# Further rows as plain-type products in four column tiles, their gate/up product between the high and the low down products, and weight loads that wait for a product

## The chip, the cores and the metric

The kernel runs on one core of one Trainium2 chip. The metric is the time of one execution on the device, in microseconds, as the median of several runs. The engines are TensorE (PE; its weight loads are shown as PEld), VectorE (DVE), ScalarE (ACT), GpSimd (POOL) and SyncE (SP), which here only issues transfers.

## The reference

One decoder layer on 1024 tokens of width 1024: forgetting attention with 16 heads, a residual with LayerNorm, and a mixture of 64 routed experts and one shared one, cut here to what the change touches:

```python
# router: sigmoid scores, 4 of 8 groups, 8 of 64 experts a token, weights scaled by 2.5
# expert e, on the tokens routed to it:
h = silu(x @ w_gate[e]) * (x @ w_up[e])      # 1024 -> 256
y = (h @ w_down[e]) * weight                 # 256 -> 1024
# shared expert: the same with ws_gate, ws_up, ws_down, on all tokens
x = layer_norm(alpha * x + shared + sum_of_routed, g, b)
```

All inputs, outputs and weights are float32.

## The kernel before, in words

**The stages.** Attention, output projection with LayerNorm and router, then the shared expert in eight blocks of 128 tokens, then the 64 routed experts in order, then the last placing of rows and the second LayerNorm. Each routed expert takes one block of 128 token rows; tokens beyond that come in *further* blocks of XR = 32 rows. With this data 31 of the 64 experts have one further block and 33 have none (`nx` is 1 or 0). The code for more than one is there and is skipped.

**The products.** The first 128 rows are computed in a split form: weights and rows are each a high and a low part of type fp32r, and a product is three matmuls, high·high, low·high, high·low. `gate_up` has 24 matmuls of 512 columns (L1032, L1035, L1038), `down` has 12 (`down_hi` L1059, L1060, then `down_lo` L1067). ScalarE makes the high parts of the weights (L1404), VectorE the low parts (L1926). Before the change the further rows use the same split weights: `xo` (and `ho`) hold the high part of the rows in columns 0 to 31, the low part in 32 to 63 and zeros behind, so one matmul gives both; `gate_up_further` has 16 matmuls (L1091, L1092), `down_further` 8 (L1109, L1110). Halves are then added by ScalarE and VectorE (`further_half` L1499, `further_sum`, `further_y_half`, `further_y`).

**The order of one expert e on TensorE.** With a further block in expert e-1: turn_h (L1046, transposes of the hidden rows of the block before), gate_up, turn_h_further (L1100), the transposes of the next rows (L1022), down_further. Then, with a further block in e: turn_further (L1081), down_hi and down_lo of the block before, gate_up_further. Without it: down_hi and down_lo only. ScalarE, in its own order: L1499 for the further block before, ht_hi (L1440), silu of the further rows (L1503), four casts of the gate/up weights of set e+2 (L1404), ho (L1507), silu (L1436), the next rows (L1432), the copy of the further result, xo (L1494), two casts of down weights, and `scale_rows` (L1452), which scales the block's result out of `k_ps`. At every even expert ScalarE, VectorE and TensorE load block counts from memory into registers (`load_counts`, L1522 on ScalarE).

**The loads.** Weights of set s (0 the shared expert, s = e+1 for expert e) are loaded in six pieces of 512 KB by SyncE: four of gate/up (L500) and two of down (L505), into two buffers each. A piece is issued when VectorE is done with the piece in the same buffer:

```python
load_gate_up(par, *(... w_gate, w_up), lambda k: sp.wait_ge(S["g_lo_ok"], G_PIECES * (s - 2) + k + 1))
load_down(par, ..., lambda k: sp.wait_ge(S["d_lo_ok"], D_PIECES * (s - 2) + k + 1))
```

GpSimd gathers the 128 (and 32) token rows of an expert by index (L664, L677) and adds the results back into memory (L689, L699). Each engine runs its experts in a loop of two experts a turn, apart from the first and last ones on some engines.

`gate_sums` (L812), which the rows below show, is an older part of the kernel: 20 plain float32 matmuls of 256 or 128 columns and 16 output rows, in four column tiles of TensorE, which hold two, four, six and eight of them (384, 896, 1408 and 1920 columns).

Of the kernel before, what the change touches and what calls it, by code (L numbers as in the profile page):

```python
# [84 lines left out]
I32 = mybir.dt.int32  # L85
U32 = mybir.dt.uint32
# [9 lines left out]
def build(nc, x, w_in, b_f, w_out, ln1_g, ln1_b, router, router_bias, w_gate, w_up, w_down, ws_gate, ws_up,  # L96
          ws_down, ln2_g, ln2_b, out):
    with ExitStack() as ctx:
# [135 lines left out]
        with ExitStack() as m:  # L234

            raw_gu = [sb(f"raw_gu{i}", [P, 2, DC, FF], c=m) for i in range(2)]
# [4 lines left out]
            xo = sb("xo", [P, DC, P], F32R, c=m)  # L241
            ho = sb("ho", [P, FC, P], F32R, c=m)
            gu_x = sb("gu_x", [XR, 2 * FF], c=m)
            ys = [sb(f"ys{i}", [P, D], c=m) for i in range(3)]
            sg = sb("sg", [P, FF], c=m)
            hh = sb("hh", [P, FF], c=m)
            ht_hi = sb("ht_hi", [P, FC, P], F32R, c=m)
            ht_lo = sb("ht_lo", [P, FC, P], F32R, c=m)
            w_x = sb("w_x", [XR, 1], c=m)
            wcol = sb("wcol", [P, E], c=m)  # L250
            gidx = [sb(f"gidx{i}", [P, 1], I32, c=m) for i in range(3)]
            sidx = [sb(f"sidx{i}", [P, 1], I32, c=m) for i in range(3)]
            sb("to_64_bytes", [P, 8], c=m)
            split = []
# [3 lines left out]
            tab = sb("tab", [P, TAB], I32, c=m)  # L258
            tok_f = sb("tok_f", [P, 1], c=m)
            tok_x = sb("tok_x", [2 * XR, 1], c=m)  # L260
        with ExitStack() as f:

            fin0 = sb("fin0", [P, TT, D], c=f)
            y_hi = sb("y_hi", [P, D], F32R, c=f)
            y_lo = sb("y_lo", [P, D], F32R, c=f)
            tokens = sb("tokens", [P, T], c=f)
            x_place = sb("x_place", [2 * XR, T], F32R, c=f)
# [12 lines left out]
            sb("up_to_the_other_set", [P, 19240], c=f)  # L280
            fin1 = sb("fin1", [P, TT, D], c=f)

# [3 lines left out]
        for n in ("masks xt_ps xt_hi_ok xt_lo_ok wf_in wf_ok gate_ps g1_in gate_step zexp_ok"  # L286
# [7 lines left out]
                  " ht_lo_ok downed scaled w_ok x_in x_turned x_rows_hi_ok x_rows_lo_ok x_w_ok x_gated x_half x_sum x_silu_ok x_h_ok x_ht_ps x_ht_hi_ok x_ht_lo_ok"  # L294
                  " x_downed x_y_half x_scaled ax_ok ax_stored summed"
                  " stands std_ok var_ok place_step y_hi_ok f_placed f_pair f_mean f_var f_std f_scaled f_step f_xg f_out").split():
# [52 lines left out]
        def g_piece(w, k):  # L349

            return tuple(a[:, k // 2, (k % 2) * 4:(k % 2) * 4 + 4, :] for a in (raw_gu[w], split[w][0], split[w][1]))

        def d_piece(w, k):
            return tuple(a[:, k, :] for a in (raw_dn[w], split[w][2], split[w][3]))

# [31 lines left out]
        def _(sp):  # L387
# [106 lines left out]
            def load_gate_up(par, gate, up, left):  # L494

                for k in range(G_PIECES):
                    left(k)
                    chunks = slice(k % 2 * (DC // 2), (k % 2 + 1) * (DC // 2))
                    w = (gate, up)[k // 2].rearrange("(p c) n -> p c n", c=DC)[:, chunks]
                    sp.dma_start(raw_gu[par][:, k // 2, chunks], w).then_inc(g_raw[par][k // 2], 16)  # L500
# [6 lines left out]
            def next_gate_up(s, par):  # L507

                load_gate_up(par, *(w[ds(s - 1, 1)].rearrange("o k n -> (o k) n") for w in (w_gate, w_up)),
                             lambda k: sp.wait_ge(S["g_lo_ok"], G_PIECES * (s - 2) + k + 1))  # L510

            def next_down(s, par):
                load_down(par, w_down[ds(s - 1, 1)].rearrange("o k n -> (o k) n"),
# [28 lines left out]
            for b in range(2, SH):  # L542
# [5 lines left out]
                elif b == 5:  # L548
                    next_gate_up(2, 0)
                elif b == 6:  # L550
                    next_down(2, 0)
# [3 lines left out]
            sp.dma_start(tab[:], tab_dram.rearrange("(p n) o -> p (n o)", p=P)).then_inc(S["c_loads"], 16)  # L555


            next_gate_up(3, 1)
# [4 lines left out]
            next_gate_up(E, 0)  # L563
            next_down(E - 1, 1)
            next_down(E, 0)

# [11 lines left out]
            for t in range(2):  # L578
                load_sums(0, t)
# [1582 lines left out]
```

## Time and profile before

| | |
|---|---|
| median of 3 runs | 1641.52 us (1641.01 to 1644.18) |
| the profiled execution | 1632.95 us, span 1631.3 us, mean clock of TensorE 0.979 |
| TensorE busy | 1574.2 us, 97% of the span |
| VectorE, ScalarE, GpSimd busy | 1183.2, 1033.3, 505.7 us |
| expert stage | from about 744 to 1568 us, then some 63 us |
| moved by the DMA queues | 368.63 MB |

An engine that waits in order for semaphores is shown idle, and the one that released it is named. TensorE's matmuls are pipelined: the starts of two neighbours are 0.227 us apart in a 512-column product, while each is shown as 0.39 us long; so starts are what to read. Times in the rows are microseconds from the start of the span, unless marked ns.

### The profile page before, as it was taken

What the parts mean: (1) busy time and instruction counts of PE and PEld (TensorE: products, weight loads), DVE (VectorE), ACT (ScalarE), POOL (GpSimd) and SP (SyncE); (2) the same over time, 40 slices, a digit from 0 to 9 for tenths busy, and PEclk for the clock granted to TensorE, in tenths of its full rate; (3) what the DMA queues carried; (4) which work ended last, traced back from release to release, by engine and by line L of the source; (5) the groups of instructions that cost most, each with busy time, mean ns of one, the idle gap of its engine ahead of it and who ended that gap; (6) DMA issues with size and microseconds to landing.
All of it is one profiled execution on the core that took longest, in us unless ns stands there. A gap on an engine that the chain in (4) does not pass through costs nothing.

```text
span 1631.3 us, 32225 instructions
## 1 busy us (share of the span) xinstructions
PE 1574.2 (97%) x8262; PEld 1310.3 (80%) x8263; DVE 1183.2 (73%) x2038; ACT 1033.3 (63%) x1709; POOL 505.7 (31%) x495
## 2 busy tenths in 40 slices
PE   6999999999999999899999999999999999999987
PEld 6997888888887788788888888788888888888864
DVE  4215777777777788838777888767876787888856
ACT  3215666666666645427667877766776777877855
POOL 0000000000000135532544454543554455454426
PEclk9999999999999999899999999999999999999995
DMA  7223222212223524568999999999998999999987
GB/s 247 91 82 96 67 59 65 71 45 71 58 65 111 185 108 170 196 218 315 318 303 309 304 363 360 329 289 263 331 322 276 286 356 326 348 365 370 366 252 283
DMA packets 161319, 368.63 MB, mean 226 GB/s; under 512 B 53008, under 2 KB 73488, under 8 KB 161264
## 3 DMA queue, kind: packets, MB, share of 16 engines
q1 hardware_dynamic: 136272, 284.21, 49.9%
q0 software_dynamic: 24992, 83.73, 19.8%
q8 instruction: 28, 0.46, 0.1%
q14 instruction: 27, 0.22, 0.0%
HBM read 294.39 MB, written 65.11 MB: 220 GB/s over the span
## 4 chain that ended last, share of the span: by engine, by line
PE 78%; DVE 7%; issue 4%; ACT 3%; DMA 3%; ACTq 2%; POOL 1%; SPq 0%; DVEq 0%; POOLq 0%
PE bank_pair L1032 6%; PE bank_pair L1035 6%; PE bank_pair L1038 6%; PE q_ps L91 4%; PE out_ps L923 4%; PE q_ps L93 4%; PE q_ps L92 4%; PE k_ps L901 4%; PE out_ps L1091 4%; PE out_ps L1092 3%; PE q_ps L1022 3%; PE k_ps L1059 3%; PE k_ps L1060 2%; PE k_ps L1067 2%; DVE gu_lo L1926 2%
## 5 line engine op out<-in xcount | busy, mean ns | idle before, releaser
L1926 DVE TENSOR_TENSOR gu_lo<-raw_gu,gu_hi 128x1024 fp32r<-128x1024 f32 x260 | 306.4, 1219 | 28.7 <-ACT gu_hi L1404 28.7
L1404 ACT CAST gu_hi<-raw_gu 128x1024 fp32r<-128x1024 f32 x260 | 253.3, 1050 | 6.0 <-DMA raw_gu<-in_moe_w_up_dram 6.0
L1032 PE MATMUL bank_pair<-gu_hi,xb_hi 128*128 128x512 f32 x576 | 235.5, 409 | 5.4 <-DVE gu_lo L1926 4.2
L1035 PE MATMUL bank_pair<-gu_lo,xb_hi 128*128 128x512 f32 x576 | 229.1, 398 | 0.0
L689 POOL DMA_INDIRECT sums_scratch<-ys,sidx x63 | 119.8, 1902 | 151.7 <-DMA sums_scratch<-ys,sidx 110.6
L1926 DVE TENSOR_TENSOR dn_lo<-raw_dn,dn_hi 128x1024 fp32r<-128x1024 f32 x130 | 152.6, 1213 | 2.2 <-ACT dn_hi L1404 1.7
L1038 PE MATMUL bank_pair<-gu_hi,xb_lo 128*128 128x512 f32 x576 | 142.7, 390 | 0.0
L1032 PEld LDWEIGHTS bank_pair<-gu_hi,xb_hi 128*128 128x128 f32 x576 | 111.5, 194 | 29.5 <-issue 6.5
L1309 ACT CAST pt_hi<-k_ps 128x512 fp32r<-128x512 f32 (+1 forms) x192 | 85.9, 482 | 74.2 <-PE k_ps L901 73.4
L620 POOL IOTA e<- 128x64 f32 x1 | 0.2, 185 | 426.6 <-DVE xs L1722 426.6
L1404 ACT CAST dn_hi<-raw_dn 128x1024 fp32r<-128x1024 f32 x130 | 130.0, 1051 | 3.2 <-DMA raw_dn<-in_moe_w_down_dram 3.2
L1035 PEld LDWEIGHTS bank_pair<-gu_lo,xb_hi 128*128 128x128 f32 x576 | 111.0, 193 | 21.6
L1038 PEld LDWEIGHTS bank_pair<-gu_hi,xb_lo 128*128 128x128 f32 x576 | 108.0, 188 | 22.9 <-DVE xb_lo L1930 0.5
L664 POOL DMA_INDIRECT x_rows<-rows_scratch,gidx x64 | 74.7, 1167 | 148.2 <-DVE wcol L1942 117.5
L1700 DVE TENSOR_TENSOR pt_lo<-k_ps,pt_hi 128x512 fp32r<-128x512 f32 (+1 forms) x192 | 100.3, 550 | 27.5 <-ACT pt_hi L1309 26.6
L1059 PE MATMUL k_ps<-dn_hi,ht_hi 128*128 128x512 f32 x288 | 118.4, 411 | 0.0
L1060 PE MATMUL k_ps<-dn_lo,ht_hi 128*128 128x512 f32 x288 | 112.5, 391 | 0.0
L91 PE MATMUL q_ps<-xt_hi,wqk_hi 128*128 128x512 f32 x256 | 108.8, 425 | 0.0
L1298 ACT ACTIVATE probs<-bank_pair,nm 128x512 f32<-128x512 f32 (+3 forms) x128 | 74.9, 587 | 42.4 <-DVE nm L1693 29.0
L1091 PE MATMUL out_ps<-gu_hi,xo 128*128 128x512 f32 x248 | 97.2, 392 | 4.5 <-DVE xo L1946 4.5
L93 PE MATMUL q_ps<-xt_hi,wqk_lo 128*128 128x512 f32 x256 | 100.2, 391 | 0.0
L92 PE MATMUL q_ps<-xt_lo,wqk_hi 128*128 128x512 f32 x256 | 100.0, 391 | 0.0
(306 smaller groups left out, 3971.5 us busy)
## 6 DMA issues: line engine op xcount, KB each, us to landing
raw_gu<-in_moe_w_gate_dram SPq DMA_DIRECT2D x128, 512.0 KB, 6.6
raw_gu<-in_moe_w_up_dram SPq DMA_DIRECT2D x128, 512.0 KB, 9.1
raw_dn<-in_moe_w_down_dram SPq DMA_DIRECT2D x128, 512.0 KB, 8.9
wqk<-in_fox_w_in_dram SPq DMA_DIRECT2D x66, 128.0 KB, 2.4
v_scratch<-v_out SPq DMA_DIRECT2D x32, 256.0 KB, 2.8
va<-v_scratch SPq DMA_DIRECT2D x16, 512.0 KB, 4.7
fin<-sums_scratch SPq DMA_DIRECT2D x16, 512.0 KB, 9.0
xs<-in_x_dram SPq DMA_DIRECT2D x8, 512.0 KB, 7.8
```

Of the source, the lines that this page charges most:

```text
L91: pe.matmul(out, w_hi, m_hi, start=start, stop=False, skip_group_check=True)
L92: pe.matmul(out, w_hi, m_lo, start=False, stop=False, skip_group_check=True)
L93: return pe.matmul(out, w_lo, m_hi, start=False, stop=stop, skip_group_check=True)
L689: g.indirect_dma_start(out=sums[0], out_offset=bass.IndirectOffsetOnAxis(ap=sidx[par][:, 0:1], axis=0), in_=ys[par][:], in_offset=None, co ...
L1032: i = pe.matmul(o3, xb_hi[s][:, c], g_hi[:, :, c], start=c == 0, stop=False, skip_group_check=True)
L1035: pe.matmul(o3, xb_hi[s][:, c], g_lo[:, :, c], start=False, stop=False, skip_group_check=True)
L1038: i = pe.matmul(o3, xb_lo[s][:, c], g_hi[:, :, c], start=False, stop=c == DC - 1, skip_group_check=True)
L1059: pe.matmul(k_ps[:, r], ht_hi[:, c], d_hi[:, c, r], start=c == 0, stop=False, skip_group_check=True)
L1060: pe.matmul(k_ps[:, r], ht_hi[:, c], d_lo[:, c, r], start=False, stop=False, skip_group_check=True)
L1091: pe.matmul(o3, xo[:, c], g_hi[:, :, c], start=c == 0, stop=False, skip_group_check=True)
L1404: a.copy(hi, raw).then_inc(S[done], 1)
L1926: dve.tensor_tensor(lo, raw, hi, ALU.subtract).then_inc(S[lo_ok], 1)
```

## The change

The further rows are no longer split. `xo` and `ho` are float32 with 32 columns, the weights are read unsplit from the load buffers, and each product is cut over four column tiles of 32 output rows: gate and up, each in even and odd chunks of the inner dimension; for down two chunks by two halves of the columns. `gate_up_further` stands between `down_hi` and `down_lo`. VectorE's low parts of the further rows are gone; the adds of halves are two of half the width. Since unsplit weights are now read late, gate/up load buffers are three, and two waits are added on SyncE, `gu_spent` (counted by TensorE in its first low down product of an expert with a further block, in its first high one without) and `downed`. The memory for the third buffer comes from tiles that are shared: hh becomes sg, the third `ys` lies in `x_rows2`, and the index table is int16, copied by GpSimd from the third up buffer. The loops of TensorE, ScalarE, VectorE and SyncE have six experts a turn, ten turns, with the first two and last two experts outside.

```diff
-            raw_gu = [sb(f"raw_gu{i}", [P, 2, DC, FF], c=m) for i in range(2)]
+            raw_gu = [[sb(f"raw_{n}{i}", [P, DC, FF], c=m) for n in ("gate", "up")] for i in range(2)]
...
-            xo = sb("xo", [P, DC, P], F32R, c=m)
-            ho = sb("ho", [P, FC, P], F32R, c=m)
+            xo = sb("xo", [P, DC, XR], c=m)
+            ho = sb("ho", [P, FC, XR], c=m)
...
+        def raw_place(s):
+
+            return s if s < 2 else (0, 2, 1)[(s - 2) % 3]
...
+        ROUND = 6
+        ROUNDS = (E - 4) // ROUND
...
+            def next_gate_up(s, place):
+
+                if place > 3:
+                    sp.wait_ge(S["gu_spent"], s - 3)
+                    stand(sp)
...
+            def next_down(s, place):
+                if place > 2:
+                    sp.wait_ge(S["downed"], SH + s - 2)
+                    stand(sp)
...
-            with sp.Fori(0, E // 2 - 2) as i:
-                for par in range(2):
-                    next_gate_up(2 * i + (par + 4), par)
-                    next_down(2 * i + (par + 3), 1 - par)
...
+            with sp.Fori(0, ROUNDS) as i:
+                for u in range(ROUND):
+                    next_gate_up(ROUND * i + (u + 4), u + 4)
+                    next_down(ROUND * i + (u + 3), u + 3)
...
-                for c in range(DC):
-                    pe.matmul(o3, xo[:, c], g_hi[:, :, c], start=c == 0, stop=False, skip_group_check=True)
-                    i = pe.matmul(o3, xo[:, c], g_lo[:, :, c], start=False, stop=c == DC - 1, skip_group_check=True)
+                for c in range(0, DC, 2):
+                    for j in range(4):
+                        i = pe.matmul(out_ps[x_tile(j), BANK:BANK + FF], xo[:, c + j // 2], raw[j % 2][:, c + j // 2], start=c == 0,
+                                      stop=c == DC - 2, skip_group_check=True)
...
+            def down_further(e, s, x, by_rows=True):
+
+                raw = raw_dn[s % 2]
+                pe.wait_ge(S["x_ht_ok"], x + 1)
+                pe.wait_ge(d_raw[s % 2], 8 * D_PIECES * (e + 1 - s % 2) + 16 * D_PIECES)
+                stand(pe)
+                for j in range(4):
+                    c, half = (j // 2, j % 2) if by_rows else (j % 2, j // 2)
+                    i = pe.matmul(out_ps[x_tile(j), BANK:T], ho[:, c], raw[:, c, HALVES[half]], start=True, stop=True, skip_group_check=True)
...
-                    down(m - 1, par, e + 1)
+                    down_hi(m - 1, par, e + 1)
+                    if not last:
+                        gate_up_further(u + 1, xi + nx - 1)
+                    down_lo(m - 1, par, spent=not last)
...
-                a.copy(gu_x[:], out_ps[XR:2 * XR, BANK:T]).then_inc(S["x_half"], 1)
+                a.copy(gu_x[:, 0:FF], out_ps[x_tile(2), BANK:BANK + FF]).then_inc(S["x_half"], 1)
+                a.copy(gu_x[:, FF:2 * FF], out_ps[x_tile(3), BANK:BANK + FF]).then_inc(S["x_up_half"], 1)
```

**On TensorE**, in the code of an expert with a further block, after its transposes (k_ps takes the down product of the block before, out_ps the further rows). Before:

```order
L1081 MATMUL bank_pair<-ident,x_rows 128x32 x8
L1054 REGISTER_ALU
L1056 REGISTER_ALU
L1059 MATMUL k_ps<-dn_hi,ht_hi 128x512
L1060 MATMUL k_ps<-dn_lo,ht_hi 128x512
...
L1067 MATMUL k_ps<-dn_hi,ht_lo 128x512 x4
L1091 MATMUL out_ps<-gu_hi,xo 128x512
L1092 MATMUL out_ps<-gu_lo,xo 128x512
```

and now:

```order
L1120 MATMUL bank_pair<-ident,x_rows 128x32 x8
L1094 MATMUL k_ps<-dn_hi,ht_hi 128x512
L1097 MATMUL k_ps<-dn_lo,ht_hi 128x512
...
L1130 MATMUL out_ps<-raw_gate,xo 32x256
L1130 MATMUL out_ps<-raw_up,xo 32x256
L1104 MATMUL k_ps<-dn_hi,ht_lo 128x512 x4
L1239 UNCONDITIONAL_BRANCH
```

The pairs at the "..." repeat, four of the down product in both, and eight of L1130, which stood as eight pairs L1091, L1092 behind L1067 before. L1067 (now L1104) ends the part.

**On SyncE**, in the loop over the experts' loads, between gate/up of one set and down of the set before. Before:

```order
L500 DMA raw_gu<-in_moe_w_up_dram 128x1024 [waits g_lo_ok]
L514 ISA
L505 ISA [waits d_lo_ok]
L505 DMA raw_dn<-in_moe_w_down_dram 128x1024
L514 REGISTER_ALU
L505 ISA [waits d_lo_ok]
L505 DMA raw_dn<-in_moe_w_down_dram 128x1024
L510 ISA
L500 ISA [waits g_lo_ok]
L500 DMA raw_gu<-in_moe_w_gate_dram 128x1024
```

and now:

```order
L523 DMA raw_up<-in_moe_w_up_dram 128x1024 [waits g_lo_ok]
L540 REGISTER_ALU
L543 ISA [waits downed]
L528 ISA [waits d_lo_ok]
L528 DMA raw_dn<-in_moe_w_down_dram 128x1024
L543 REGISTER_ALU
L528 ISA [waits d_lo_ok]
L528 DMA raw_dn<-in_moe_w_down_dram 128x1024
L536 ISA [waits gu_spent]
L523 ISA [waits g_lo_ok]
L523 DMA raw_gate<-in_moe_w_gate_dram 128x1024
```

The order of the loads is the same; a wait for `downed` now stands ahead of the down pieces and one for `gu_spent` ahead of the gate/up pieces. They are issued in the order down of set s, then gate/up of set s+2, both after the end of expert s-2.

## Rows read from the trace of the kernel before

**Rows 1.** The page, part 1: busy us (share of the span) xinstructions.
```profile
PE 1574.2 (97%) x8262; PEld 1310.3 (80%) x8263; DVE 1183.2 (73%) x2038; ACT 1033.3 (63%) x1709; POOL 505.7 (31%) x495
```

**Rows 2.** Windows: stretch, us, busy of five engines, PEclk, DMA share, GB/s.
```profile
764.00:1567.00 803.00, 790.90 (x3826) 652.14 (x3826) 630.84 (x786) 587.23 (x757) 382.45 (x363) 1.00 1.00 327
1484.80:1542.40 57.60, 56.57 (x278) 47.50 (x277) 50.71 (x58) 48.59 (x59) 25.20 (x23) 1.00 1.04 367
1590.00:1620.00 30.00, 28.57 (x64) 16.47 (x63) 21.25 (x38) 18.00 (x27) 25.96 (x12) 0.58 0.71 280
```

**Rows 3.** Timeline of PE: start us, us, operation, count [idle before].
```profile
1032.92 0.39 PE L1046 MATMUL bank_pair<-ident,hh 128*128 128x128 f32 x2
...
1206.32 0.39 PE L1091 MATMUL out_ps<-gu_hi,xo 128*128 128x512 f32 x1
...
1209.95 0.39 PE L1046 MATMUL bank_pair<-ident,hh 128*128 128x128 f32 x2
...
1217.01 0.48 PE L1109 MATMUL out_ps<-dn_hi,ho 128*128 128x512 f32 x1
...
1219.04 1.06 PE L1081 MATMUL bank_pair<-ident,x_rows 32*128 32x32 f32 x8
...
1226.52 0.39 PE L1046 MATMUL bank_pair<-ident,hh 128*128 128x128 f32 x2
```

**Rows 4.** Groups of 764:1567: shapes xcount, busy us, mean ns, idle before.
```profile
L1091 PE MATMUL out_ps<-gu_hi,xo 128*128 128x512 f32 x240 | 94.0, 392 | 4.5 <-DVE xo L1946 4.5
```

**Rows 5.** Waits of 764:1567: us in total, times, longest us.
```profile
ACT gu_x L1499 <- PE out_ps L1092: 73.0, 30, 3.3
...
ACT ht_hi L1440 <- issue: 27.5, 13, 2.3
...
PEld out_ps L1091 <- DVE xo L1946: 6.6, 5, 1.5
```

**Rows 6.** Timeline of PE around gate_sums.
```profile
71.27 0.28 PE L93 MATMUL bank_pair<-wv_hi,xt_lo 128*128 128x256 f32 x1
71.48 3.44 PE L812 MATMUL q_ps<-upto,gate 128*16 128x256 f32 x40
74.84 0.39 PE L91 MATMUL bank_pair<-wv_hi,xt_hi 128*128 128x256 f32 x1
75.07 0.28 PE L92 MATMUL bank_pair<-wv_lo,xt_hi 128*128 128x256 f32 x1
```

**Rows 7.** Timeline of ACT in three experts.
```profile
1033.40 1.12 ACT L1452 ACTIVATE ys<-k_ps,wcol 128x1024 f32<-128x1024 f32 x1
1036.58 0.37 ACT L1440 CAST ht_hi<-bank_pair 128x256 fp32r<-128x256 f32 x1 [2.06 <-issue]
...
1206.77 1.12 ACT L1452 ACTIVATE ys<-k_ps,wcol 128x1024 f32<-128x1024 f32 x1 [0.94 <-PE k_ps L1067]
1210.15 0.58 ACT L1499 COPY gu_x<-out_ps 32x512 f32<-32x512 f32 x1 [2.26 <-PE out_ps L1092]
...
1211.80 3.89 ACT L1404 CAST gu_hi<-raw_gu 128x1024 fp32r<-128x1024 f32 x4
1216.20 0.21 ACT L1507 CAST ho<-out_ps 128x64 fp32r<-128x64 f32 x1 [0.51 <-PE out_ps L1100]
```

**Rows 8.** Timeline of SP's queue: start us, us of issuing.
```profile
1206.69 1.47 SPq L505 DMA_DIRECT2D raw_dn<-in_moe_w_down_dram  x2
1214.29 1.43 SPq L500 DMA_DIRECT2D raw_gu<-in_moe_w_gate_dram  x2
```

**Rows 9.** Instruction queues (page, part 3), and one wait of 690:800.
```profile
q8 instruction: 28, 0.46, 0.1%
q14 instruction: 27, 0.22, 0.0%
...
PEld bank_pair L1046 <- issue: 1.0, 1, 1.0
```

**Rows 10.** Waits of 1567:1632.
```profile
POOL fin L783 <- DMA fin<-sums_scratch: 9.0, 3, 8.2
```

More of the change, by code:

```diff
@@ L85 @@
 I32 = mybir.dt.int32
+I16 = mybir.dt.int16
 U32 = mybir.dt.uint32
@@ L492, in _, with load_gate_up @@
                 weights_out(t - 1)
[L494 removed]
+            def load_gate_up(place, gate, up, left):
                 for k in range(G_PIECES):
@@ L1170, in _, with expert @@
                     logits(TT - 1)
-            def expert(e, par, last=False):
+            def expert(e, u, last=False):
+                par = u % 2
                 w = 1 - par
@@ L1215, in expert @@
                         turn_h_further(xi + nx - 1)
-                        down_further(w, e + 2, xi + nx - 1)
+                        down_further(e, u + 1, xi + nx - 1, by_rows=False)
                         put_in_place(True)
                 with pe.If(nx < 1):
-                    down(m - 1, par, e + 1)
+                    down_hi(m - 1, par, e + 1, spent=not last)
+                    down_lo(m - 1, par)
                     if last:
@@ L1224, in expert @@
                 return xi, nx
-            with pe.Fori(0, E // 2 - 1) as i:
-                for par in range(2):
-                    expert(2 * i + par, par)
-            expert(E - 2, 0)
-            expert(E - 1, 1, last=True)
+            for e in range(2):
+                expert(e, e)
+            with pe.Fori(0, ROUNDS) as i:
+                for u in range(2, ROUND + 2):
+                    expert(ROUND * i + u, u)
+            expert(E - 2, E - 2)
+            expert(E - 1, E - 1, last=True)
         @block.scalar
@@ L1597, in _ @@
             expert(1, 1, "", counts)
-            with act.Fori(1, E // 2 - 1) as i:
-                counts = load_counts(2 * i)
-                for par in range(2):
-                    expert(2 * i + par, par, "", counts)
+            with act.Fori(0, ROUNDS) as i:
+                for u in range(2, ROUND + 2):
+                    if u % 2 == 0:
+                        counts = load_counts(ROUND * i + u)
+                    expert(ROUND * i + u, u, "", counts)
             counts = load_counts(E - 2)
-            expert(E - 2, 0, "", counts)
-            expert(E - 1, 1, "last", counts)
+            expert(E - 2, E - 2, "", counts)
+            expert(E - 1, E - 1, "last", counts)
             for t in range(TT):
@@ L2014, in load_counts, with expert @@
                 return [dve.value_load(earlier[0:1, ds(e + k, 1)], min_val=0, max_val=E * TAB_BLOCKS) for k in range(4)]
-            def expert(e, par, counts, last=False):
+            def expert(e, u, counts, last=False):
+                par = u % 2
                 m = SH + e
```

225 lines of the change are left out of this document (119 added, 106 removed).

## The prediction

> **What bounds the kernel now.** I read first the busy shares on the page, then the windows of the expert stage, then the waits there, and last single timelines. TensorE is busy 97% of the span [rows 1]. In 764 to 1567 us, 61 experts, it is busy 790.9 of 803.0 us at clock 1.00, so what it issues is what the stage costs; the DMA engines read 1.00 there too, at 327 GB/s [rows 2]. An expert starts with the transposes of its hidden rows (L1046). With a further block before it and in it, one lasts from 1209.95 to 1226.52, 16.57 us [rows 3]. Six without a further block take 57.6 us [rows 2], 9.6 each. Thirty-one of the 64 experts have one further block of 32 rows; 30 fall in this window, as the counts of L1091 (240 = 30 x 8) show [rows 4].
>
> The waits are to be read with that: the long ones belong to engines with time to spare. ScalarE waits 73.0 us in 30 times for L1092, then VectorE for ScalarE. TensorE waits for almost nothing: 6.6 us of weight loads for VectorE's low parts of the further rows [rows 5]. So shorter TensorE work pays only until the spare time of ScalarE and of the DMA queues is used up, and that is where I look.
>
> **What is taken from TensorE.** gate_up_further was 16 matmuls of 512 columns: it starts at 1206.32 and the next expert's work at 1209.95, 3.63 us. down_further is 8 at the same pace: from 1217.01, 8 x 0.227 = 1.8 us, and with the slow first ones 2.03 by the start of the next transposes, 1219.04 [rows 3]. Now they are plain-type matmuls, 16 of 256 columns and 4 of 512, in four column tiles of 32 rows. The trace has one place with that shape: gate_sums (L812), where 20 plain matmuls stand in four column tiles, the longest tile holding seven of 256 columns and one of 128, 1920 columns. It takes 3.44 us from 71.48, and the next product begins at 74.84 [rows 6]. All four tiles hold 384 + 896 + 1408 + 1920 = 4608 columns; one after the other at the longest tile's pace that would be about 8 us, so the tiles run side by side, and a column costs 3.36 / 1920 = 1.75 ns in its tile. The gate/up block has 4 x 256 columns a tile: 1.79 us. The down block has 512: 0.90. To each I add about 0.25 us for changing over: before L812 a gap of 0.09 more than the pace, after it a first product of 0.39 against 0.28 us. So 2.03 for 3.63 and 1.15 for 2.03: 2.48 us for each of 30, **-74.4 us**. VectorE's low parts of xo go as well, and the five waits for them: **-4.5** by TensorE's idle time [rows 4].
>
> The Trainium skill, "TensorEngine Tiling (Array Packing)", section on performance, speaks against taking the ideal: changing tile modes drains the array, and quoted speed-ups stay under the number of tiles. This trace agrees in kind (the slow first product of rows 6). Its page "TensorE: Matmul & The Clock Gate" gives 2.38 for three column tiles; were four tiles to give about 3 of 4, an estimate from that page, the two blocks would cost 2.4 and 1.2 us with the changeover counted in, and 12 us of the gain would go.
>
> **What ScalarE gets in return.** Before, the last low down products come ahead of gate/up of the further rows, so the scaling of the result rows (L1452, 1.12 us) runs at 1206.77, 3.2 us before the expert ends, under the further products; then ScalarE waits 2.26 us for them [rows 7]. Now down_lo stands last, and L1452 can start only some 0.45 us into the next expert, as it does already where no further block is: 1033.40, with that expert's start at 1032.92 [rows 3, 7]. Behind it stand, in ScalarE's order: the loads of four block counts into registers in every even expert (from the end of L1452 to L1440 2.06 us at 1036.58, in all 27.5 us in 13 times [rows 5, 7]); the half copies of gate/up; the high part of the hidden rows; silu; four casts of gate/up weights, 3.89 us; and only then ho, the turned further hidden rows, for which down_further waits. Ho starts at 1216.20, 6.25 us into the expert, and TensorE wants it at 1217.01, 7.06 us in [rows 3, 7]. After: L1452 ends at 0.45 + 1.12 = 1.57; register loads to 3.65; from the half copy to the first cast is 1.65 us (1210.15 to 1211.80) and the second half copy adds 0.1; the casts end at 5.4 + 3.89 = 9.3; ho at 9.5 (its wait for TensorE's transposes is gone by then). That is 2.3 us late, less what the register loads overlap with: I take 1.9. Of the 30 experts with a block before them 17 are even; in the other 13 ho comes at 7.45, 0.4 late. 17 x 1.9 + 13 x 0.4 = **+38**. Bounds: nothing where TensorE is late for another reason (0), and 17 x 2.4 + 13 x 0.6 = 49.
>
> **What the loads get.** Before, SyncE issued gate/up loads piece by piece as the splits finished, from 1214.29, 4.3 us into an expert, and down loads one expert earlier than they are wanted (1206.69) [rows 8]. Now gate/up for set s waits for gu_spent (the first low down product, the end of expert s-4; a third buffer makes up for it), and down for set s waits for the end of expert s-2, and its cast comes in expert s-1. Behind these waits in SyncE's queue stand only the next loads. Six 512 KB loads are issued in one burst, and down has one expert, less its last 4 us, to land. The bytes: 803 us x 327 GB/s = 263 MB in 61 experts, 4.3 MB each; in 1484.80 to 1542.40 the queues moved 367 GB/s [rows 2]. At that pace 4.3 MB need 11.7 us. On the whole 263 MB fit in 716 us, well under what I forecast; only runs of experts without further blocks, 17 experts in all, ask for more than the queues give, and live on loads issued early. With less issued early, up to 17 x (11.7 - 9.6) = 36 us could come back. The lower bound is 0, since ScalarE's delays lengthen the neighbours; I take a quarter: **+9**.
>
> **The longer loops.** From two experts a turn to six, ten turns. The kernel before fetched 28 + 27 instruction packets in its whole run, and one wait, 1.0 us with no other cause, stands at the start of its loop, L1046 [rows 9]. If a turn has one such stall, it is 10 x 1.0 = **+10**; the bounds are 0 and the rival below.
>
> The rest I cost at nothing: int16 copy of the table on GpSimd, under shared-expert blocks in which its gathers are early; one DVE operation fewer, one more, both under TensorE's 97%. At the end nothing is gained from the last block: the final loads and GpSimd's wait of 9.0 us for them [rows 10] set that part, with the clock at 0.58 [rows 2].
>
> Sum: -74.4 - 4.5 + 38 + 9 + 10 = -22. The profiled execution took 1632.95 us (span 1631.3), the median is 1641.52, 8.6 above; I take the difference off the median: **1619.5 us**.
>
> **Rivals.** (a) The full gain: the queue and ScalarE waits vanish in one another, the loops stay resident: -79, 1563 us. For it: the DMA average leaves room, and TensorE, when it waits for ho, still has eight transposes to do. Against it: ScalarE's order is fixed, and its chain above has no slack. 0.10. (b) The loads bound it: +36 in place of +9, and ho at its upper 49: -79 + 36 + 49 + 10 = +16 as a sum of both uppers, but they overlap in time, so nearer -5 to +5, 1637 to 1646. For it: DMA share 1.00. 0.12. (c) The other side: the loop body of six experts no longer stays in TensorE's instruction store, and each turn fetches it anew. Place: TensorE between two turns and at each jump over a skipped block. Price: 1.0 us for each stall [rows 9]; with eight a turn +80 for +10, so +48, 1690 us. It decides from 32 us of stalls, 3.2 us a turn. For it: three times the instructions a turn. Against: in straight code before 744 us only one such wait is seen. 0.15. The Trainium skill, "Runtime: NRT & Kernel Launch", section on instruction fetch mechanics, says TensorE holds 128 KiB of instructions and that a jump outside what is held stalls; by it six experts would be near or above the limit, two were not. No run here shows the limit. (d) The column tiles don't run side by side: 16 x 0.45 and 4 x 0.9 us in place of 2.03 and 1.15, +7.6 us for each of 30, about +230 against the forecast, near 1850 us. Against it stands all of rows 6. 0.03.
>
> **The numbers.** The forecast has 0.60, with 1600 to 1636 of its own. A change under 0.2% (3.3 us) can't be told from none here. Faster: forecast 0.60, (a) 0.10, half of (b) 0.06. Same: 0.04 of (b). Slower: (c), (d) and the rest of (b). The range from 1583 to 1652 leaves out (a)'s far end, (d), and most of (c).
>
> **What the profile after would show.** The L1130 group: about 1.8 us a block from its start, then k_ps products at once; L1150 about 0.9. L1452 right after an expert's start everywhere. TensorE waiting for ho before L1150, near 2 us in even experts. ScalarE's wait for the further products of 73.0 us gone. DMA above 335 GB/s in the stage. Instruction packets: if many more than 55, (c). I am wrong if ho is hidden, or if waits for raw_dn show in ScalarE by tens of us.

## The result, and the profile after

The change made the kernel slower: 1791.13 us (1785.8 to 1799.69) against 1641.76 us beside it, a ratio of 1.091 [1.086, 1.096]. The prediction was 1619.5 us, faster.

The page of the changed kernel: its span, the busy time, the granted clock by slices, and the two instruction queues.

```profile
span 1785.6 us, 33142 instructions
...
PE 1572.1 (88%) x8758; PEld 1242.8 (70%) x8759; DVE 1182.0 (66%) x2036; ACT 1031.0 (58%) x1741; POOL 431.1 (24%) x496
...
PEclk9999999999999988998998999998899989888996
...
q8 instruction: 147, 2.41, 0.5%
q14 instruction: 123, 1.01, 0.2%
```

Four things are to be seen beside [rows 1, 9]. TensorE is busy about as long as before (1572.1 against 1574.2 us) although it was given some 75 us less to do. Its idle time went from 57 to 214 us. The clock row has many eights where it had nines; its mean is 0.934 against 0.979. And the two instruction queues moved 147 and 123 packets where they had moved 28 and 27. The window of the expert stage says the same beside [rows 2]: the DMA queues move 278 GB/s, not 327, so they are not what holds it.

```profile
764.00:1700.00 936.00, 778.68 (x4250) 577.50 (x4248) 620.72 (x777) 575.23 (x776) 300.55 (x359) 0.91 0.88 278
```

The waits of that stretch (who waited, for whom, us in total, times, the longest) beside [rows 5]:

```profile
ACT ys L1499 <- PE k_ps L1104: 156.4, 43, 8.4
...
PEld bank_pair L1081 <- issue: 92.5, 51, 7.3
...
PE bank_pair L1081 <- issue: 72.4, 42, 6.9
...
PEld k_ps L1094 <- issue: 59.5, 17, 6.7
ACT x_rows L1547 <- issue: 45.9, 17, 7.3
...
PEld bank_pair L1120 <- issue: 27.4, 15, 6.3
```

TensorE's weight loads waited 92.5, 59.5 and 27.4 us for "issue": for nothing that the profile knows, no product, cast or transfer. Its products stood idle for 72.4 us of the first of these (the PE line), and for 24.1 and 14.2 us of the other two. ScalarE's 45.9 us at L1547 are such waits too, together with its register loads. Single waits are long, up to 7.3 us. One on the timeline of the weight loads, with the idle time ahead of it in the last bracket:

```profile
1213.08 0.29 PEld L1094 LDWEIGHTS k_ps<-dn_hi,ht_hi 128*128 128x128 f32 x1 [6.72 <-issue]
```

L1094 is the first product of down_hi, behind the branches round a further block that this expert does not have. The profile names nothing that it still needed. That the instruction itself was missing is the reading that the experiments test.

### The profile page after: what moved, and what is told of

It reads as the page before. It is cut to its first block, busy times and chain, and to the rows that moved or that the text cites. A ratio compares the mean times of both kernels' runs of the same rounds, so it can differ in the third digit from the quotient of the medians.

```text
span 1785.6 us, 33142 instructions
## 1 busy us (share of the span) xinstructions
PE 1572.1 (88%) x8758; PEld 1242.8 (70%) x8759; DVE 1182.0 (66%) x2036; ACT 1031.0 (58%) x1741; POOL 431.1 (24%) x496
## 4 chain that ended last, share of the span: by engine, by line
PE 69%; issue 11%; DVE 8%; DMA 5%; ACT 4%; ACTq 1%; SPq 1%; another core or an unknown queue 1%; DVEq 0%; POOL 0%; POOLq 0%
PE bank_pair L1067 6%; PE bank_pair L1070 6%; PE bank_pair L1073 5%; PE out_ps L958 4%; PE k_ps L1094 4%; PE q_ps L92 4%; PE k_ps L1104 4%; PE q_ps L94 4%; PE q_ps L93 4%; PE k_ps L936 4%; PE k_ps L1097 3%; PE out_ps L1130 3%; DMA raw_up<-in_moe_w_up_dram 3%; PE q_ps L1057 3%; ACT gu_hi L1451 2%
## 5 line engine op out<-in xcount | busy, mean ns | idle before, releaser
L1067 PE MATMUL bank_pair<-gu_hi,xb_hi 128*128 128x512 f32 x576 | 254.5, 442 | 2.8 <-DVE gu_lo L1978 1.5
L1070 PE MATMUL bank_pair<-gu_lo,xb_hi 128*128 128x512 f32 x576 | 245.4, 426 | 8.2 <-issue 8.2
L1978 DVE TENSOR_TENSOR gu_lo<-raw_gate,gu_hi 128x1024 fp32r<-128x1024 f32 x130 | 153.6, 1223 | 34.9 <-ACT gu_hi L1451 32.4
L1094 PE MATMUL k_ps<-dn_hi,ht_hi 128*128 128x512 f32 x288 | 129.3, 449 | 45.7 <-issue 24.1
L1499 ACT ACTIVATE ys<-k_ps,wcol 128x1024 f32<-128x1024 f32 x63 | 70.3, 1116 | 161.1 <-PE k_ps L1104 157.2
L1978 DVE TENSOR_TENSOR gu_lo<-raw_up,gu_hi 128x1024 fp32r<-128x1024 f32 x130 | 158.3, 1219 | 7.5 <-ACT gu_hi L1451 7.4
L1067 PEld LDWEIGHTS bank_pair<-gu_hi,xb_hi 128*128 128x128 f32 x576 | 123.0, 214 | 29.7 <-issue 3.3
L720 POOL DMA_INDIRECT sums_scratch<-ys,sidx x63 | 107.1, 1700 | 150.0 <-ACT ys L1499 76.5
L1451 ACT CAST dn_hi<-raw_dn 128x1024 fp32r<-128x1024 f32 x130 | 129.8, 1049 | 11.5 <-DMA raw_dn<-in_moe_w_down_dram 6.4
L1451 ACT CAST gu_hi<-raw_up 128x1024 fp32r<-128x1024 f32 x130 | 129.6, 1046 | 11.1 <-DMA raw_up<-in_moe_w_up_dram 11.0
L1451 ACT CAST gu_hi<-raw_gate 128x1024 fp32r<-128x1024 f32 x130 | 130.0, 1050 | 7.0 <-DMA raw_gate<-in_moe_w_gate_dram 5.5
L1094 PEld LDWEIGHTS k_ps<-dn_hi,ht_hi 128*128 128x128 f32 x288 | 59.0, 205 | 72.0 <-issue 59.9
L1081 PE MATMUL bank_pair<-ident,sg 128*128 128x128 f32 x144 | 36.9, 343 | 79.6 <-issue 73.6
```

The source lines that it names most:

```text
L720: g.indirect_dma_start(out=sums[0], out_offset=bass.IndirectOffsetOnAxis(ap=sidx[par][:, 0:1], axis=0), in_=ys[par][:], in_offset=None, co ...
L1067: i = pe.matmul(o3, xb_hi[s][:, c], g_hi[:, :, c], start=c == 0, stop=False, skip_group_check=True)
L1070: pe.matmul(o3, xb_hi[s][:, c], g_lo[:, :, c], start=False, stop=False, skip_group_check=True)
L1094: i = pe.matmul(k_ps[:, r], ht_hi[:, c], d_hi[:, c, r], start=c == 0, stop=False, skip_group_check=True)
L1451: a.copy(hi, raw).then_inc(S[done], 1)
L1978: dve.tensor_tensor(lo, raw, hi, ALU.subtract).then_inc(S[lo_ok], 1)
```

## The experiments

The instruction counts below are counted in the built programs, a split-type product or transpose as two instructions (its weight load and its product) and a plain-type product as four, as the trace shows it. The "store theory" of the expectations is rival (c) of the prediction: an engine keeps its recent instructions in a store, and a loop body that is too large for it is fetched again in every turn. For the loop bodies over the experts:

| kernel | TensorE | ScalarE | VectorE |
|---|---|---|---|
| before | 745 | 145 | 165 |
| changed | 2625 | 435 | 493 |

The packets of the first instruction queue (q8) can be set against the size of TensorE's whole program: 28 packets for 7312 instructions before, 34 for 8772 with four experts a turn (experiment 3), 32 for 8319 in the small kernel (experiment 5). That is some 260 instructions a packet, and in these three kernels all code came once.

**1. TensorE without the code of a second further block.** Code that never runs with this data is taken out of the changed kernel:

```diff
-                    with pe.If(nx > 1):
-                        with pe.Fori(0, nx - 1) as k:
...
```

> The changed kernel without TensorE's code for a second or later further block of one expert (no expert of this data has one, so no executed product is left out; the other engines keep theirs). Instructions in TensorE's six-expert loop body, by my count of the built programs: 2625 in the changed kernel, 1941 here, 745 in the kernel before. Store theory (TensorE's loop body no longer stays resident and is fetched anew every turn): if the size that stays resident lies above 1941, instruction packets fall from 270 to near 60-70, TensorE's waits with no cause (92.5 + 59.5 + 27.4 us of weight loads) fall below 20 us, the clock returns to about 0.98, and the time is 1600 to 1640. Load theory (the late weight loads delay the splits and these delay TensorE): nothing changes, 1780 to 1800. Tile theory (plain-type column tiles cost more than I took): nothing changes either.

Measured: 1732.84 us, ratio to before 1.055 [1.053, 1.056]. That is 60 us less than the changed kernel relative to before. Of what is executed only one branch an expert with a further block is gone (31 instructions in all), no product and no load, so neither the load theory nor the tile theory allows it. That branch jumped over the code taken out; this experiment alone does not tell the size of the body from the jump, the next two do. The waits for an instruction at L1094 fell from 59.5 to 20.4 us and at L1120 from 27.4 to 12.9, where the skipped code had stood; those at L1081 rose, from 92.5 to 106.9. The instruction queues are hardly emptier, where I had expected 60 to 70 packets in all:

```profile
q8 instruction: 125, 2.05, 0.5%
q14 instruction: 123, 1.01, 0.2%
```

So the case of a limit above 1941 instructions fell, and with it the 1600 to 1640 us that I had expected; the theory needed a body small enough.

**2 and 3. The kernel before, TensorE's loop at six and at four experts a turn.** Nothing else differs, no product, load or order:

```diff
-            with pe.Fori(0, E // 2 - 1) as i:
-                for par in range(2):
-                    expert(2 * i + par, par)
+            for par in range(2):
+                expert(par, par)
+            with pe.Fori(0, 10) as i:
+                for u in range(2, 8):
+                    expert(6 * i + u, u % 2)
```

> The kernel before, with TensorE's expert loop alone cut into six experts a turn, ten turns, the first two experts outside; all else as before. Its loop body has 2229 instructions by my count. Store theory: slower than before, with long waits of TensorE that have no cause and over 150 instruction packets, by 60 to 150 us, if the limit lies between 1941 and 2229. Load theory and tile theory: the same time as before within 0.5%, since neither loads nor products differ.

> The kernel before, with TensorE's expert loop cut into four experts a turn, fifteen turns: 1487 instructions by my count. Store theory: within 0.3% of before, 55 to 65 instruction packets. A rival within it (the number of experts a turn or the longer straight code costs in itself, by each jump): slower, about two thirds of what six a turn cost.

Six a turn (2229 instructions): 1712.49 us, ratio 1.043 [1.040, 1.046]. Four a turn (1487): 1645.55 us, ratio 1.003 [1.001, 1.005]. Both are as the store theory had them. The pages of six and of four:

```profile
span 1711.0 us, 32148 instructions
...
q8 instruction: 127, 2.08, 0.5%
q14 instruction: 27, 0.22, 0.0%
```

```profile
q8 instruction: 34, 0.56, 0.1%
q14 instruction: 27, 0.22, 0.0%
```

Six a turn moved 99 packets more than before, all on one queue, which is thus TensorE's. The program itself is longer by 2202 instructions, some nine packets; the other 90 are ten for each of the nine times that the loop returns to its start. Four a turn moved 34, no more than its code once. The long waits (3.8 to 6.9 us) stand where the loop turns, shorter ones at later transposes that begin an expert:

```profile
PEld bank_pair L1046 <- issue: 66.3, 21, 6.9
```

This shows the mechanism alone: +69 us from the size of a loop body. The jumps round skipped code are the same in all three kernels, and cost nothing that shows while the body is small. For TensorE the limit lies between 1490 (experiment 5) and 1941 instructions.

**4. The kernel before with gate_up_further between down_hi and down_lo,** in the split form:

```diff
-                    down(m - 1, par, e + 1)
+                    down_hi(m - 1, par, e + 1)
+                    if not last:
+                        gate_up_further(w, xi + nx - 1)
+                    down_lo(m - 1, par)
...
-                    gate_up_further(w, xi + nx - 1)
+                        gate_up_further(w, xi + nx - 1)
```

> The kernel before with gate_up_further of the split form moved between down_hi and down_lo, nothing else. By my prediction's term for ScalarE: the scaling of the result rows (L1452) and the register loads behind it come after the start of the next expert, ho comes 1.9 us late in 17 even experts and 0.4 in 13 odd ones, so 38 us slower, with TensorE waiting for ho before L1109. If that term is wrong: within 0.3% of before.

Measured: 1746.46 us, ratio 1.062 [1.060, 1.065], +103 us where I expected 38. TensorE's waits for ho are there, 30 of them, and each is 1.8 us on the average:

```profile
PE out_ps L1109 <- DVE ho L1964: 54.9, 30, 2.6
```

That is 54.9 us of the 103. Most of the rest can be seen on TensorE's timeline around one of them, and in the windows of the same stretch (PEclk is the third value from the end):

```profile
1206.63 0.79 PE L1109 MATMUL out_ps<-dn_hi,ho 128*128 128x512 f32 x1 [2.61 <-DVE ho L1964]
...
1207.64 0.63 PE L1109 MATMUL out_ps<-dn_hi,ho 128*128 128x512 f32 x1
1208.07 0.63 PE L1110 MATMUL out_ps<-dn_lo,ho 128*128 128x512 f32 x1
...
1212.75 0.39 PE L1059 MATMUL k_ps<-dn_hi,ht_hi 128*128 128x512 f32 x1
1212.98 0.40 PE L1060 MATMUL k_ps<-dn_lo,ht_hi 128*128 128x512 f32 x1
```

```profile
1200.00:1204.00 4.00, 4.00 (x22) 3.08 (x20) 2.62 (x4) 3.47 (x6) 0.87 (x2) 1.00 0.77 125
1204.00:1207.60 3.60, 0.99 (x3) 0.83 (x3) 3.60 (x6) 2.94 (x5) 0.00 (x0) 0.76 0.62 170
1207.60:1212.50 4.90, 4.90 (x13) 3.79 (x12) 2.49 (x4) 1.97 (x3) 1.19 (x2) 0.50 0.88 289
1212.50:1223.00 10.50, 10.50 (x52) 8.79 (x51) 8.98 (x10) 8.53 (x11) 6.57 (x6) 0.99 0.83 253
```

After 3.6 us in which TensorE did little, the clock is 0.50 (1.2 GHz) for 4.9 us: products follow each other at 0.43 us and not 0.23, and then it is whole again. Over the run, the mean clock is 0.953 against 0.979. The clock is granted at 1.2 or 2.4 GHz, so time at half clock is twice the missing share, 2 x 0.047 x 1745.7 = 164 us against 2 x 0.021 x 1631.3 = 69; half of the 95 us more is lost, 48 us. The two profiled executions are 114.4 us apart, since that of before was one of the shorter ones: TensorE's idle time grew by 67.9 us, of which the waits for ho are 54.9, and its busy time by 46.5, near the 48. The remaining 13 us of idle time were not followed up.

**5. The changed kernel made small.** The code of a second further block is out on three engines, and TensorE has one copy of an expert's first half in place of two:

```diff
+                turn_h(m - 1)
+                pe.wait_ge(S["g_lo_ok"], G_PIECES * (e + 2))
+                gate_up(par, w, "rows_", m + 1)
                 with pe.If(before_it > 0):
-                    turn_h(m - 1)
-                    pe.wait_ge(S["g_lo_ok"], G_PIECES * (e + 2))
-                    gate_up(par, w, "rows_", m + 1)
                     pe.wait_ge(S["ht_lo_ok"], m)
                     turn_h_further(xi - 1)
-                    turn_next()
+                turn_next()
+                with pe.If(before_it > 0):
                     down_further(e - 1, u, xi - 1)
-                with pe.If(before_it < 1):
...
```

> The changed kernel with its six experts a turn, made small: code for a second further block left out on TensorE, ScalarE and VectorE (never executed with this data), and TensorE's two copies of the first half of an expert made one, with two branches round the further parts. My count of loop bodies: TensorE 1490 (was 2625; 1487 stayed resident in the kernel before with four a turn), ScalarE 314 (435), VectorE 355 (493). Products, loads and orders are those of the changed kernel. Store theory: packets near 60 to 80, waits without cause gone, 1610 to 1650 us. If the further cost is the order on ScalarE and the clock that answers each of its waits: packets near 60 to 80 too, but 1650 to 1700 us, with TensorE waits for ho before L1150 and a clock of 0.96. Load theory: over 1720 us.

Measured: 1704.53 us, ratio 1.037 [1.032, 1.042], in none of the three bands that I had expected. TensorE's queue is down to its code once, the other is not:

```profile
q8 instruction: 32, 0.52, 0.1%
q14 instruction: 75, 0.61, 0.1%
```

And there VectorE stands still, for nothing, with TensorE behind it (the timelines of VectorE and of TensorE, and the waits):

```profile
1037.88 0.42 DVE L1981 TENSOR_TENSOR x_rows<-out_ps,x_rows 32x256 f32<-32x256 f32 x1 [12.44 <-issue]
```

```profile
1039.82 0.41 PE L1139 MATMUL out_ps<-ident,x_rows 32*128 32x32 f32 x2 [6.62 <-DVE x_rows L1989]
```

```profile
DVE x_rows L1981 <- issue: 60.5, 7, 13.0
DVE ht_lo L1969 <- issue: 42.3, 5, 13.2
```

On VectorE's timeline one such wait comes with each turn of the loop: nine of them, 4.0 to 13.2 us long, 10.9 on the average. The further cost was not the order on ScalarE, to which I had given 1650 to 1700 us, but the next engine's loop body, which was too large too.

**6 and 7. The order.** gate_up_further behind down_lo, in the small kernel and in the changed one; gu_spent is counted by the first transpose of the next expert:

```diff
-                    down_hi(m - 1, par, e + 1)
+                    down(m - 1, par, e + 1)
                     if not last:
                         gate_up_further(u + 1, xi + nx - 1)
-                    down_lo(m - 1, par, spent=not last)
```

> The small kernel with six experts a turn, and gate_up_further again behind down_lo, as before the change; gu_spent is then counted by the first transpose of the next expert's hidden rows, right after it. Order theory (the place between the down products makes ho late, and each wait lowers the clock for a stretch): no waits for ho, clock 0.98 or more, 30 to 60 us faster than the small kernel in the changed order, 1570 to 1600 us. If order costs nothing in the plain type, whose ho has no low part to wait for: within 5 us of the small kernel in the changed order. Load theory: both over 1700 us.

> The changed kernel with gate_up_further behind down_lo, its large loop bodies kept. Store theory: still 240 or more instruction packets and long waits without cause; 1740 to 1800 us. If the order were the main cause: under 1700 us.

Small kernel 1709.19 us (1.039 [1.035, 1.042]), changed kernel 1785.07 us (1.085 [1.081, 1.088]). Both pairs agree within their intervals (1.037 and 1.039; 1.091 and 1.085), and the 1570 to 1600 us that I had expected of the small kernel in this order did not come. The changed kernel's 1785.07 lies in the 1740 to 1800 of the store theory. With the stalls there, the order tells nothing either way.

**8 and 9. VectorE small as well,** in both orders: one copy of an expert with three branches, 261 instructions in the loop where the small kernel had 355.

```diff
                 with dve.If(before_it > 0):
                     further_sum(xi - 1)
-                    h_lo(m - 1)
+                h_lo(m - 1)
+                with dve.If(before_it > 0):
                     further_h(xi - 1)
-                    next_weights(range(G_PIECES - 1))
...
+                next_weights(range(G_PIECES - 1))
...
```

> The small kernel with six experts a turn, in the changed order, and now VectorE's two copies of an expert made one as well: 261 instructions in its loop body by my count (355 in the small kernel, whose VectorE stood still without cause for 12 to 13 us about once a turn, 102.8 us in 12 waits of the expert stage; 165 in the kernel before). Store theory, now for VectorE: those waits go, the second instruction queue falls from 75 packets to near 27, the clock rises, and the time is 1590 to 1630 us. If those waits have another cause (an event not shown, a transfer): still near 1700 us.

> The same with gate_up_further behind down_lo. By my term for ScalarE's order it should be 10 to 40 us faster than its twin in the changed order, 1565 to 1600 us; if the order costs nothing in the plain type, within 5 us of it.

In the changed order 1624.18 us, ratio 0.994 [0.992, 0.997]; behind down_lo 1613.33 us, ratio 0.986 [0.982, 0.989]. The page of the first:

```profile
span 1621.1 us, 32689 instructions
...
PEclk9999999999999999899999999999999999999995
...
q8 instruction: 32, 0.52, 0.1%
q14 instruction: 29, 0.24, 0.0%
```

Both queues are back at 32 and 29 packets. In these two kernels no loop body is fetched anew. The first is the changed kernel with the executed products, loads and orders that I had predicted for it. Its time is 4.7 us from the predicted 1619.5, but that is in part luck: this set of runs had a kernel before of 1637.20 us, so the gain is 13 us where 22 was predicted, 32 without the term for the loops. The order is worth 10.9 us here, at the lower end of the 10 to 40 that I expected, and the time behind down_lo, 1613.33, is above the band of 1565 to 1600.

**10 and 11. The kernel before, with VectorE's or ScalarE's loop alone at six a turn** (the edit of experiment 2 on that engine; 487 and 423 instructions).

> The kernel before with VectorE's expert loop alone at six experts a turn, ten turns (487 instructions by my count, 165 before); all else as before. Store theory: VectorE stands still without cause once a turn, over 40 more packets in the second instruction queue, 60 to 130 us slower. Otherwise: within 0.5% of before.

> The kernel before with ScalarE's expert loop alone at six experts a turn, ten turns (423 instructions by my count, 145 before; 435 in the changed kernel). Store theory: the second queue gains 40 or more packets and ScalarE stands still once a turn, 40 to 130 us slower. Otherwise: within 0.5% of before.

1689.73 us, 1.032 [1.029, 1.034], and 1688.1 us, 1.031 [1.027, 1.035]. The second instruction queue, for VectorE and then for ScalarE, with the waits:

```profile
q14 instruction: 76, 0.61, 0.1%
```

```profile
DVE gu_x L1952 <- issue: 42.7, 7, 7.7
```

```profile
q14 instruction: 74, 0.61, 0.1%
```

```profile
ACT gu_x L1499 <- issue: 48.9, 9, 8.3
```

That is five packets for each return of the loop on one small engine, with the few that the longer code takes once set aside. The timelines show one long wait for each, 6.1 to 8.8 us on VectorE and 5.6 to 8.3 on ScalarE, 7.0 and 7.1 on the average; TensorE's long ones in experiment 2 were 5.6 on the average, with shorter ones behind them. On either engine six a turn costs three quarters of the 69 us that it costs on TensorE. ScalarE's time lies in the band that I had expected (40 to 130 us), VectorE's +53 just under its 60 to 130.

**12. Three edits against what is left,** on the kernel of experiment 8:

```diff
-                        next_gate_up(m, e, u + 2)
+                        next_gate_up(m, e, u + 2, range(3) if further_too else range(G_PIECES))
                     if further_too:
                         further_turned_h(xi - 1)
+                        if pos != "last":
+                            next_gate_up(m, e, u + 2, range(3, G_PIECES))
...
+                coming = load_counts(e + 1) if ahead else None
                 rows_before()
...
-                    sp.wait_ge(S["downed"], SH + s - 2)
+                    sp.wait_ge(S["oproj"], TT + s - 1)
```

(oproj, whose earlier use is over at 8, is counted on by the first products of down_hi.)

> The kernel with all loop bodies small and gate_up_further between the down products, with three edits against the waits that are left: ScalarE casts ho behind three of the four gate/up casts, it loads the next pair's block counts ahead of the scaling of the result rows (within a turn, two of three pairs), and the down loads wait for the first down product behind down_further rather than for the end of the expert. If ho and the register loads are what TensorE waits for there (20.0 us in 19 times at L1150) and the late down loads cost ScalarE 14.0 us: 1585 to 1612 us. If the loads' bandwidth sets it (six loads, gather and add of an expert at 360 to 370 GB/s in the runs without further blocks): 1612 to 1625 us, no better than its base.

1618.33 us (1612.52 to 1621.15), ratio 0.983 [0.981, 0.985], the best ratio with experiment 9. It beats its base by 1.1 points; its time is in the band that I had given to the loads, its ratio is not at its base's. TensorE's waits for ho fell from 20.0 us to 1.8 and ScalarE's for raw_dn from 14.0 to 7.3; in return its waits at the gate/up product of the further rows rose from 6.7 us to 21.7 (15.2 for VectorE's rows, 6.5 for ScalarE's xo). Which of the three edits did how much was not tried apart.

## Why the prediction was wrong

The prediction was 1619.5 us, with a range from 1583 to 1652, and 1791.13 is above all of it and above rival (c)'s 1690. **The step that failed** is "The longer loops": "If a turn has one such stall, it is 10 x 1.0 = +10". The rival (c) named the mechanism, with 0.15, but only on TensorE, at 1.0 us a stall. Three things were off.

It is three engines. Alone in the kernel before, the longer loop costs 1712.49 - 1643.14 = +69 us on TensorE, 1689.73 - 1637.20 = +53 on VectorE, and 1688.10 - 1637.20 = +51 on ScalarE. With everything else of the change, 1624.18 - 1637.20 = -13, the sum is +160; measured was 1791.13 - 1641.76 = +149. The sum is near, but it does not prove that nothing else is in it: the changed body on TensorE has 2625 instructions, not 2229, and taken off one after the other the effects are 60 us (TensorE to 1941), 30 (TensorE to 1490 and ScalarE to 314) and 73 (VectorE to 261). What an engine's stall costs thus depends on the stalls of the others; how they fall on each other was not followed up.

It is not 1.0 us. The one stall of [rows 9] came once, and never again at that size in a body that stayed. A body that does not stay is fetched anew, ten packets a turn for TensorE, and what is waited for is up to 6.9 us there, 7.0 us on the average on VectorE in the kernel before, and 10.9 in the small one (12.44 at 1037.88). My argument against (c), that in straight code before 744 us only one such wait is seen, was misread and is no argument. The wait of [rows 9] stands at 764.00, in the loop, at the third expert, where the loop returns for the first time; and in the straight code ahead there are waits for "issue" of up to 1.9 us. That code took 22 of the 28 packets of TensorE's queue without a long wait behind the start, so straight code says little about a jump back. I had sized the price from the only row there was and did not widen it.

And the clock answers. A lower clock is in [rows 2] as a number (0.58 at the end, where TensorE had waited shortly before), but no term of the sum had it. In the changed kernel, behind the wait that ends at 1213.08, the clock reads 0.56 for the next 6.9 us. Over its whole run 2 x 0.066 x 1785.6 = 236 us run at half clock against 69 before, so that some 84 us of the loss are not waiting at all; this is why TensorE's busy time did not fall, though it had some 75 us less to do.

The Trainium skill, "Runtime: NRT & Kernel Launch", section on instruction fetch mechanics, gives 2048 instructions for TensorE, 512 for the others, and a stall at a jump out of what is held. The runs agree on the stall; on the size they say less: bodies of 1941 on TensorE, of 423 on ScalarE and of 355 on VectorE were fetched every turn, 1490, 314 and 261 were not. By the page's figures 1941 on TensorE should have stayed, and of the changed kernel only TensorE's 2625 was too large; had I trusted them, ScalarE and VectorE would still have been costed at nothing. Beside the page, these limits decide, for the bodies as they lie in these programs; whether the same body in another place of the program would stay was not tried.

**The other steps**, in the kernel of experiment 8, where they can be read:

*The products.* The last product ahead of a gate/up block of the further rows, its first product and the one behind it; then the same for a down block, with the transposes ahead of it:

```profile
1052.95 0.39 PE L1097 MATMUL k_ps<-dn_lo,ht_hi 128*128 128x512 f32 x1
1053.38 0.38 PE L1130 MATMUL out_ps<-raw_gate,xo 128*32 128x256 f32 x1
...
1055.24 1.20 PE L1104 MATMUL k_ps<-dn_hi,ht_lo 128*128 128x512 f32 x4
```

```profile
1023.87 1.16 PE L1057 MATMUL q_ps<-ident,x_rows 128*128 128x128 f32 x8
1024.96 1.06 PE L1150 MATMUL out_ps<-raw_dn,ho 128*32 128x512 f32 x8
1025.96 0.50 PE L1094 MATMUL k_ps<-dn_hi,ht_hi 128*128 128x512 f32 x1
1026.29 0.39 PE L1097 MATMUL k_ps<-dn_lo,ht_hi 128*128 128x512 f32 x1
```

The blocks take 1.86 and 1.00 us from their first product to the next one. My 2.03 and 1.15, from gate_sums [rows 6], hold the changeover at both ends. With it, in undisturbed cases, 0.09 us ahead of gate/up (0.32 against the pace of 0.23), 0.18 ahead of down (1.09 against the 0.91 of the kernel before) and 0.10 behind each, they are 2.05 and 1.28. So a block saves 2.33 us where I had 2.48, and 30 of them 70 us where I had 74.4. The term was nearly right: 4 us of the gain went, not the 12 that the estimate by the Trainium skill's 2.38 would have taken. The draining that the prediction cites from "TensorEngine Tiling (Array Packing)" stands there under "Key Properties" and not in the section on performance, and the speed-ups under the number of tiles stand in "TensorE: Matmul & The Clock Gate". The four tiles run side by side, which puts rival (d) out.

*ScalarE.* I had +38 for ho. In the plain type TensorE waits 20.0 us, half of it, in 19 times; in the split form, with ho's low part in the chain, 54.9 us and again the clock. The mechanism was right, its size in the plain type too large, and ScalarE's register loads are there, at 1.5 us where I had 2.0 (26.1 us in 17 times). The first line shows them, the last the 8.0 us of TensorE that the total below takes up:

```profile
ACT x_rows L1536 <- issue: 26.1, 17, 1.9
...
ACT gu_hi L1440 <- DMA raw_up<-in_moe_w_up_dram: 21.1, 16, 2.7
...
PE out_ps L1150 <- ACT ho L1545: 20.0, 19, 3.0
...
ACT dn_hi L1440 <- DMA raw_dn<-in_moe_w_down_dram: 14.0, 15, 3.0
...
PE bank_pair L1081 <- issue: 8.0, 14, 1.1
```

*The loads.* ScalarE waits 21.1 and 14.0 us for weights. The start of the first of six experts without a further block, and the start behind the last of them:

```profile
1488.63 0.50 PE L1081 MATMUL bank_pair<-ident,sg 128*128 128x128 f32 x2
...
1557.89 0.50 PE L1081 MATMUL bank_pair<-ident,sg 128*128 128x128 f32 x2 [1.21 <-DVE sg L1965]
```

69.3 us for six, 11.5 each, where I had worked out 11.7 as the pace of the loads [rows 2]; before it was 57.6. Over all sixteen experts with a further block neither before nor in them, the mean went from 9.70 to 10.51 us, +13 for my +9. So what rival (b) says of the loads is there in the last such stretch; elsewhere it shows most in the third expert of the two stretches of three (11.93 us from 922.30, 12.08 from 1378.33, against 9.35 and 9.34 before). The queues moved 331 GB/s in the stage, not the more than 335 that I had named as a sign.

*The end* was not looked at apart.

The total without the loops came out at -13 where I had -22 - 10 = -32. Between the two profiled executions TensorE's busy time fell by 51.0 us and its idle time rose by 40.8. The idle time is about as forecast, 38 + 9 - 4.5 = 42.5, though made up otherwise: half of the waits for ho, more for the loads, and 8.0 us of products at L1081 for nothing that the profile names, ahead of which TensorE loads registers and branches. The -4.5 for VectorE's low parts did not come: TensorE still waits 6.7 us for the further rows ahead of L1130 (4.6 for VectorE, 2.1 for ScalarE). The busy time fell by less than the 70 us of the products, in good part through the clock, which no term had (0.972 against 0.979, 2 x 0.007 x 1621 / 2 = 11 us); some 8 us stay open.

## What to carry to other kernels

Count the instructions of each engine's loop body before unrolling it further, the branches that never run included: here a body too large on any one of three engines cost 3 to 4% by itself, more than the change gave with all bodies small (0.6%, or 1.4% with the other order). Code that is never executed is then not free, and one copy with two branches, which made the bodies small enough, was cheaper than two copies. A wait of TensorE has to be priced with the stretch at half clock behind it: in experiment 4 it was about as much again (55 us and 48).

## What the runs showed of the hardware that I had not expected

A loop body that does not stay is fetched anew every turn, and more than the body is fetched: ten packets of some 260 instructions for the 2229 and for the 1941 instructions of TensorE, five of half that size for the 487 and for the 355 of VectorE. VectorE, with 355 instructions in its loop, stood still for up to 13.2 us a turn, longer than any single wait of TensorE with six times as many in the kernel before (6.9 us). And a wait of 2.61 us was followed by 4.9 us at clock 0.50, with products 0.43 us apart in place of 0.23.
